# State-space outputs: the products that share a matrix are added on GpSimd before TensorE multiplies

## The reference

```python
bu = lax.complex(jnp.einsum('bsgc,gpc->bsgp', ug, b_bar.real),
                 jnp.einsum('bsgc,gpc->bsgp', ug, b_bar.imag))
_, states = lax.associative_scan(combine, (a, bu), axis=1)      # x_t = Abar x_{t-1} + Bbar u_t
y = (jnp.einsum('bsgp,gcp->bsgc', states.real, C_re)
     - jnp.einsum('bsgp,gcp->bsgc', states.imag, C_im))
y = y.reshape(bsz, seq, D_SSM) + D_skip * uf
y = jax.nn.gelu(y)
y = y * jax.nn.sigmoid(y @ w_glu + b_glu)
```

## Time and profile before

| | |
|---|---|
| median of 3 runs | 1530.39 us (1530.20 to 1530.48) |
| profiled execution | 1530.54 us |
| its span | 1528.8 us |
| PE busy | 1505.9 us, 99% |
| DVE busy | 1055.8 us, 69% |
| ACT busy | 809.7 us, 53% |
| POOL busy | 28.9 us, 2% |
| granted TensorE clock | 0.999 |

### The profile page before, as it was taken

One profiled execution on the slowest core, in us unless ns is written; L12 is line 12 of the kernel. 1 busy time (PEld: TensorE's weight loads), 2 busy tenths in 40 slices (PEclk: granted clock), 3 DMA queues, 4 the chain that ended last, 5 costly groups with the idle time before them and its releaser, 6 DMA issues.

```text
span 1528.8 us, 24067 instructions
## 1 busy us (share of the span) xinstructions
PE 1505.9 (99%) x9541; PEld 1323.3 (87%) x9541; DVE 1055.8 (69%) x1363; ACT 809.7 (53%) x1066; POOL 28.9 (2%) x58
## 2 busy tenths in 40 slices
PE   8999999999999999999999999999999999999998
PEld 8988988888888889998988888888889988888886
DVE  7999766667665666876766557666576866765666
ACT  7877653334444445766454444444445765454443
POOL 1011000000000001000000000000001000000000
PEclk9999999999999999999999999999999999999999
DMA  8432545557555666434455565465674624546653
GB/s 255 139 101 94 184 138 193 189 192 249 188 197 183 208 193 172 152 111 137 157 176 194 190 220 183 148 220 182 202 220 138 191 76 133 182 156 204 204 180 109
DMA packets 207021, 265.08 MB, mean 173 GB/s; under 512 B 14186, under 2 KB 176356, under 8 KB 206948
## 3 DMA queue, kind: packets, MB, share of 16 engines
q1 hardware_dynamic: 206884, 264.04, 54.1%
q10 hardware_dynamic: 64, 0.02, 0.0%
HBM read 262.99 MB, written 1.05 MB: 173 GB/s over the span
## 4 chain that ended last, share of the span: by engine, by line
PE 91%; DVE 6%; ACT 2%; DMA 0%; issue 0%; SPq 0%; DVEq 0%; ACTq 0%
PE bank L470 47%; PE bank L524 23%; PE bank L528 12%; DVE wl L437 2%; PE bank L2109 2%; ACT wh L430 1%; PE bank L2123 1%; PE bank L1462 1%; PE bank L2138 1%; DVE u_parts L957 1%; PE bank L1449 1%; DVE res L947 0%; DVE sq L938 0%; ACT u_parts L893 0%; PE bank L2113 0%; DVE rstd L1025 0%
## 5 line engine op out<-in xcount | busy, mean ns | idle before, releaser
L437 DVE TENSOR_TENSOR wl<-raw,wh 128x2048 fp32r<-128x2048 f32 (+4 forms) x238 | 513.6, 2170 | 180.8 <-ACT wh L430 178.9
L430 ACT CAST wh<-raw 128x2048 fp32r<-128x2048 f32 (+4 forms) x238 | 429.0, 1812 | 121.0 <-PE bank L470 117.4
L524 PE MATMUL bank<-u_parts,wh 128*128 128x512 f32 x1520 | 380.0, 392 | 0.1
L524 PEld LDWEIGHTS bank<-u_parts,wh 128*128 128x128 f32 x1520 | 276.4, 189 | 52.4 <-issue 0.8
L470 PE MATMUL bank<-u_parts,wh 128*128 128x256 f32 (+1 forms) x1344 | 252.1, 288 | 1.1 <-DVE wl L437 1.0
L528 PEld LDWEIGHTS bank<-u_parts,wl 128*128 128x128 f32 x1520 | 207.4, 190 | 14.9
L470 PEld LDWEIGHTS bank<-u_parts,wh 128*128 128x128 f32 (+1 forms) x1344 | 208.0, 190 | 6.2 <-issue 4.1
L528 PE MATMUL bank<-u_parts,wl 128*128 128x256 f32 x1520 | 211.9, 282 | 0.0
L470 PE MATMUL bank<-u_parts,wl 128*128 128x256 f32 (+1 forms) x672 | 189.6, 282 | 0.0
L470 PE MATMUL bank<-wh,hh 128*128 128x512 f32 x440 | 172.1, 391 | 0.5
L470 PE MATMUL bank<-wl,hh 128*128 128x512 f32 x440 | 171.8, 391 | 0.0
(11 more groups left out here) (374 smaller groups left out, 1789.9 us busy)
## 6 DMA issues: line engine op xcount, KB each, us to landing
raw<-ffn_wg SPq DMA_DIRECT2D x44, 1024.0 KB, 5.4
raw<-ffn_wu SPq DMA_DIRECT2D x44, 1024.0 KB, 5.4
raw<-ffn_wd SPq DMA_DIRECT2D x44, 1024.0 KB, 5.0
raw<-w_ff SPq DMA_DIRECT2D x32, 1024.0 KB, 5.3
raw<-w_in SPq DMA_DIRECT2D x28, 1024.0 KB, 6.1
raw<-w_out SPq DMA_DIRECT2D x12, 1024.0 KB, 5.0
raw<-w_gate SPq DMA_DIRECT2D x8, 1024.0 KB, 5.4
raw<-w_in SPq DMA_DIRECT2D x16, 512.0 KB, 5.3
```

The costliest lines, as they stand in the source:

```text
L430: ins = act.copy(dst, src)
L437: ins = dve.tensor_tensor(dst, src, upper.bitcast(F32), ALU.subtract)
L524: return pe.matmul(two(bank[b + f]), slab_view(wh, slot, KD, WCOLS)[:, k, f * P:(f + 1) * P], u_parts[:, k, :, :], start=k == 0, stop=Fals ...
```

## The change

GpSimd takes part in the outputs. For each state tile it makes, in place, plane 0 minus plane 3 and plane 1 plus plane 2. `pe_y` then multiplies two planes in place of four, by `c_t[0]` and `c_t[2]`, and waits for GpSimd's semaphore `turned_back` in place of VectorE's `prod_done`. `dve_split` becomes `split_slab`, which can be given any engine, and the splits of slabs 10, 13 and 15 are issued on GpSimd; they leave VectorE's list. GpSimd's list now mixes masks, pairs of additions and these splits.

```diff
+            def state_back(s):
+                p = prod[s % 4]
+                pool.wait_ge(prod_done, s + 1)
+                pool.tensor_tensor(p[:, 0, :], p[:, 0, :], p[:, 3, :], ALU.subtract)
+                pool.tensor_tensor(p[:, 1, :], p[:, 1, :], p[:, 2, :], ALU.add).then_inc(turned_back, 1)
+            state_back(0)
+            state_back(1)
+            masked(0)
+            state_back(2)
+            state_back(3)
+            masked(1)
+            state_back(4)
+            split_slab(pool, 10)
+            masked(2)
...
         def pe_y(pe, s0):
             if s0 % 4 == 0 and s0 >= 4:
                 pe.wait_ge(y_taken, s0 // 4)
-            pe.wait_ge(prod_done, s0 + 2)
+            pe.wait_ge(turned_back, s0 + 2)
-            for n, (c, q) in enumerate(((0, 0), (1, 3), (2, 2), (2, 1))):
+            for n, c in enumerate((0, 2)):
                 for s in (s0, s0 + 1):
                     j = s % 4
-                    mm = pe.matmul(bank[3][32 * j:32 * j + 32, 0:T], c_t[c][:, s, :], prod[s % 4][:, q, :], start=n == 0, stop=n == 3)
-                    if n == 3:
+                    mm = pe.matmul(bank[3][32 * j:32 * j + 32, 0:T], c_t[c][:, s, :], prod[s % 4][:, n, :], start=n == 0, stop=n == 1)
+                    if n == 1:
...
-            dve_split(dve, 9)
-            dve_split(dve, 10)
+            split_slab(dve, 9)
             dve_state(dve, 5)
```

More of the change, by code:

```diff
@@ L431, in act_round, with split_slab @@
             ins.then_inc(rounded[slot], 1)
-        def dve_split(dve, n, more=0):
+        def split_slab(eng, n, more=0):
             what, part, slot, u = slabs[n]
-            dve.wait_ge(rounded[slot], more + u + 1)
+            eng.wait_ge(rounded[slot], more + u + 1)
             for src, upper, dst in zip(slab_pieces(raw, n, False), slab_pieces(wh, n, True), slab_pieces(wl, n, True)):
-                ins = dve.tensor_tensor(dst, src, upper.bitcast(F32), ALU.subtract)
+                ins = eng.tensor_tensor(dst, src, upper.bitcast(F32), ALU.subtract)
             ins.then_inc(split[slot], 1)
@@ L1256, in keep_earlier_keys, with masked @@
                                           pattern=[[0, 2], [1, P]], channel_multiplier=-1)
-            for h in range(HEADS):
+            def masked(h):
                 pool.wait_ge(ln_done, h + 1)
@@ L1263, in b1_pool @@
                 keep_earlier_keys(at_sp).then_inc(sp_masked, 1)
+            def state_back(s):
[12 more added lines that the diff above has]
+            masked(2)
+            state_back(5)
+            masked(3)
+            state_back(6)
+            state_back(7)
+            masked(4)
+            state_back(8)
+            state_back(9)
+            split_slab(pool, 13)
+            masked(5)
+            state_back(10)
+            state_back(11)
+            split_slab(pool, 15)
+            masked(6)
+            state_back(12)
+            state_back(13)
+            masked(7)
+            state_back(14)
+            state_back(15)
         def start_vectors(eng, names):
@@ L1922, in b1_dve @@
             dve_state(dve, 1)
-            dve_split(dve, 7)
-            dve_split(dve, 8)
+            split_slab(dve, 7)
+            split_slab(dve, 8)
             dve_state(dve, 2)
@@ L2538, in b2_dve @@
             dve_rope(dve, l, 3)
-            dve_split(dve, where[("uq", l)] + 2)
+            split_slab(dve, where[("uq", l)] + 2)
             r, rot = slice(HD, QK_M), slice(QK_M, P)
@@ L2544, in b2_dve @@
                                   sin_m[rot].rearrange("p (a t) -> p a t", a=1).to_broadcast([ROPE_M, 2, T]), ALU.mult).then_inc(m_sined, 1)
-            dve_split(dve, where[("ukv", l)] + 2)
+            split_slab(dve, where[("ukv", l)] + 2)
             all_heads = lambda t_: t_[r].rearrange("p (a t) -> p a t", a=1).to_broadcast([ROPE_M, HEADS, T])
@@ L2563, in b2_dve @@
                               .to_broadcast([HEADS * N_CMP, HEADS, HD]), ALU.mult).then_inc(w2_read, 1)
-            dve_split(dve, where[("gate2", l)] + 2)
-            dve_split(dve, where[("gate2", l)] + 3)
+            split_slab(dve, where[("gate2", l)] + 2)
+            split_slab(dve, where[("gate2", l)] + 3)
             dve.wait_ge(cs_done, l + 1)
@@ L2603, in b2_dve @@
             for q in range(4):
-                dve_split(dve, where[("proj", l)] + q + 2)
+                split_slab(dve, where[("proj", l)] + q + 2)
                 dve_up(dve, where[("proj", l)], l + 1, q)
@@ L2607, in b2_dve @@
                 if q < 3:
-                    dve_split(dve, where[("out2", l)] + q + 2)
+                    split_slab(dve, where[("out2", l)] + q + 2)
             big_dve(dve, nj + 1, False, where[("out2", l)] + 5)
```

61 lines of the change are left out of this document (30 added, 31 removed).

## The result

The changed kernel takes 1540.22 us (median of 4 runs, 1539.70 to 1540.32); the kernel before, on the same chip, 1530.30 (4 runs, 1530.06 to 1530.48). The ratio is 1.0064, with a 95% interval of 1.0047 to 1.0082: slower by 9.9 us, the size and the sign forecast. The profiled execution took 1540.32 with a span of 1538.3, the one of before 1530.54 with 1528.8.

The account below looks back on a forecast made before the run. PE was taken as the bound, DVE close behind in the state-space stage. DVE's last products 8.7 us later plus 1.0 at the stage's end gave 9.7, so 1530.5 + 9.7 = 1540.2 us; range 1532 to 1546.

Parts of the forecast that it names:

- What bounds the kernel: State-space stage, 46 to 155 us: PE busy throughout, DVE 104.8 of 109 us, so both engines are at their limit.
- PE's 6.9 us: Output pairs in the state-space stage: half of 13.85 us of matmuls goes, 6.9 us less on PE.
- The lock for long instructions: Three GpSimd splits beside DVE's two-SBUF instructions: each excludes the other; DVE stands 4.35, 2.4 and 4.35 us, together 11.1.
- rival A: States 5, 10 and 12: long GpSimd instructions don't hold DVE up; −5.8 us, 1524.7, faster; chance 8%.
- The early release: GpSimd beside DVE: the lock lasts up to about 0.15 us before POOL's recorded end.
- The length of a split on GpSimd: 128x2048 split on GpSimd: 4.65 us by a straight line through additions of 256 and 384 columns.
- The end in proportion, 5.39: 128x2048 split on GpSimd: upper value, in proportion to a 384-column addition's 1.01 us, 5.39 us.
- Rival C: Slab 13: splits of 5.4 us or more and slower adds, POOL falls behind, PE waits; 1545 to 1549; 10%.
- The additions and masks: GpSimd's 16 pairs of adds cost DVE 2.1 us, behind states 1, 5, 7, 9; eight masks 3.7 more.
- DVE's last products: End of DVE's state products: −8.2 + 11.1 + 2.1 + 3.7 = 8.7 us later, at 160.9.
- The end: Last products to slab product: split 2.2, adds 1.4, two handings-over of 0.1, half pair 0.93; 4.65, 1.0 more.
- What PE would show: Profile after: PE idle before its last output pairs on POOL's adds, some 3 us each.

Follow-up runs that it names:

- Experiments 3 and 4: Kernel before plus, at the three split places, unused GpSimd subtractions of 128x2048 (1537.41 us), or five GpSimd memsets of 128x1024 each instead (1530.57 us).
- x2: Kernel before with the splits of slabs 10, 13 and 15 on GpSimd, no additions, four output matmuls a state tile: 1535.83 us, ratio 1.0034.
- x1: Changed kernel with the splits of slabs 10, 13 and 15 back on VectorE, GpSimd's additions kept: 1537.47 us, ratio 1.0043.
- x3: Kernel before plus three idle GpSimd subtractions of 128x2048 f32 at the places of the splits, results unused: 1537.41 us, ratio 1.0045.
- x5: Changed kernel, but the last output pair (states 14 and 15) takes four planes directly, without GpSimd additions: 1539.93 us, ratio 1.0059.
- the parts alone: x1, the additions without the splits on GpSimd (1537.47 us), and x2, the splits on GpSimd without the additions (1535.83 us).
- x8: x1 plus 24 idle matmuls on PE before the last output pair, where it waits: 1536.95 us, ratio 1.0045.
- x10: Changed kernel plus 24 idle matmuls before the B products of states 14 and 15, and 20 before z product 7: 1542.14 us.
- x9: x5 plus 24 idle matmuls before the B products of states 14 and 15, and 20 before z product 7: 1538.81 us, ratio 1.0057.

## Why the prediction was right

Point by point, by its own steps.

- **What bounds the kernel.** Held. DVE was so near PE that it became the bound, and nothing of PE's 6.9 us was left: it idles for 8.3 us in the stage's window and runs slower in part of the rest.
- **The lock for long instructions**, the step that no row showed. Held. DVE lost 4.80 − 0.42 = 4.38, 2.83 − 0.42 = 2.41 and 4.82 − 0.42 = 4.40, 11.2 in all, where 11.1 stood (4.35, 2.4, 4.35). Experiments 3 and 4 show the cause: the reads, with no work moved, make the kernel slower by 6.7 us (1.6 of it by the clock behind a wait), and memsets as long together, which only write, cost nothing. With the held additions in the rows above, that decides against rival A. The early release came out at 0.13 to 0.14 us before POOL's recorded end (79.30 + 4.83 = 84.13 against 79.61 + 4.38 = 83.99), close to the 0.15 taken.
- **The length of a split on GpSimd.** 4.65 by the line; 4.63 where nothing is in front (x2). The end in proportion, 5.39, was wrong, and the 4497 ns of the Trainium skill ("GPSIMD Engine Reference", section "3.1 Elementwise — side-by-side cycle accounting") are 0.13 under the measured 4.63, which in the sum is 0.4. Rival C is out: the 5.62 of slab 13 is 1.0 of wait for the phase arithmetic and a split of usual length, and PE waited for no split of POOL's.
- **The additions and masks.** 2.1 + 3.7 = 5.8 stood; 17.1 − 11.2 = 5.9 is measured. Only the sum is tested by that. One place was not as told: the phase arithmetic behind states 5 and 9 loses 1.4, where 2 × 0.5 stood.
- **DVE's last products.** 160.67 against 152.15: 8.5 later, where 8.7 stood. By the measured 17.1 and the 8.2 saved it would be 8.9. Of the 0.4 between, 0.25 come from ahead of the stage: DVE's first state starts at 45.69 in this execution and at 45.94 before, so from there on DVE is 8.8 later.
- **The end.** 160.67 to 165.25 is 4.58, where 4.65 stood; before it was 3.64. The four terms of the prediction add up to 4.73, not 4.65 (and the masks' 6 × 1.0 + 2 × 0.4 to 6.8, not 6.7), slips of 0.1 that change nothing. Half an output pair took 1.06 and not 0.93. The row of 160.76 shows the addition held up by DVE's split as the sum had it.
- **What PE would show.** Mostly wrong. I had some 3 us of idle time before each of the last output pairs, three of them. The waits are 2.1 and 1.6 us before the last two and none before the one ahead of them; another of 1.15 stands before the second pair of the stage. 4.5 us more are waits at B products (L1483, three of them), which wait for DVE as well. A start 9.5 us later with 6.9 us less to do leaves 16.4 us for PE to lose; only 9.9 of them are idle time, and most of the rest is the low clock of the next point. Since DVE set the end, the sum did not depend on how PE lost them.
- **Not in the prediction: the clock.** Behind its waits PE ran in part at the 1.2 GHz level. The windows view of the changed kernel, where the clock of before is 1.00 in both stretches:

```profile
96.00:100.00 4.00, 3.00 (x12) 2.27 (x13) 3.90 (x8) 3.52 (x5) 0.71 (x2) 0.56 0.00 0
...
148.00:152.00 4.00, 1.87 (x8) 1.19 (x9) 3.93 (x8) 2.67 (x4) 1.41 (x2) 0.50 0.00 0
```

By the chain it cost nothing here, because DVE ended later than even the slow PE. That is luck of this kernel: it cost x1, x2 and x3 some 1.5 us each and x5 all but 0.3 of its gain, and it is most of why three of my expectations (x1, x2, x5) were 1.5 to 2 us too low. The prediction came out without this term only because the term is off the chain.

What stays open: why the parts alone (+6.8 and +5.2) come to 12.0 and the whole to 9.9. The two low clocks, 3.0 us that the whole does not pay, would more than explain it, but the splits also fall at other places in x2 than in the changed kernel, and no run separates the two.

## What to carry to other kernels

Before work goes to GpSimd, ask what it reads and what VectorE does at that minute: in these traces an instruction of GpSimd that reads SBUF held up VectorE's instructions with two SBUF operands for nearly its whole length (3.1 to 4.4 us by one long one, 2.4 where PSUM readers filled the rest), and the other way about. Here a split moved away saved VectorE 2.2 us and cost it up to 4.4. Quarters, most of them placed beside VectorE's PSUM readers, cost it a third of what whole splits did, but they can come late for TensorE. Eight additions in place of 32 and three splits, where VectorE had time for them, made a kernel that is 1.7 us faster than before. And where TensorE is made to wait, count the wait and also the stretch behind it.

## What the runs showed of the hardware that I had not expected

- TensorE's granted clock falls behind waits in the middle of a busy program. In stretches of 4 us it was 0.56 of 2.4 GHz behind a wait of 2.75 us and 0.50 behind two of 1.42 and 2.13 in the changed kernel, 0.54 in x5 (1.42 and 2.77), 0.57 in x3 (3.7), 0.66 in x1 (3.13). Behind a single wait of 1.3 us it was 0.57 in x8 and 0.50 in x1. The matmuls there take 1.92 in place of 1.06 (eight) and 3.92 in place of 2.92 (24, part of them slow). It does not fall behind each such wait: the changed kernel waited 1.6 us before its last pair and kept 1.00, x10 waited 2.33 at the same place and fell to 0.67.
- Idle matmuls on constants keep the clock up (1.00 in x9 from 148 to 152, where x5 had 0.54), but they move the work behind them. x10, with the same ones, was 1.9 us slower than the changed kernel; in its profiled execution 1.55 of 2.5 us came from a fall of the clock behind a later wait.
- GpSimd's subtraction of 128x2048 f32 takes 3.60 us with a bf16 result and 4.63 with an fp32r result. The inputs differ too: one tensor read twice there, two tensors here, so which of the two makes the difference is not separated.
